# A float32 transformer kernel on one core: each 512-column matmul of the linear layers issued as two of 256 columns on the same weights

## What is computed

```python
proj = h @ w_in                                   # both mixing layers
out = mixed @ w_out
k, v = jnp.split(rms_norm(mem, mem_norm_g) @ w_kv, 2, axis=-1)      # 256 rows, not 512

def swiglu_ffn(x, norm_g, w_in, w_out):           # D_FF = 2816, four times
    gate, up = jnp.split(rms_norm(x, norm_g) @ w_in, 2, axis=-1)
    return (jax.nn.silu(gate) * up) @ w_out
```

## Time and profile before

| | |
|---|---|
| median of 3 runs | 3417.19 us (3414.03 to 3419.39) |
| profiled execution, whole | 3432.71 us |
| profiled execution, span from first to last instruction | 3430.7 us |
| PE busy | 3310.2 us, 18,526 matmuls |
| PEld busy | 2629.9 us, 18,526 weight loads |
| DVE, ACT, POOL busy | 1745.3, 1193.3, 411.6 us |
| mean granted TensorE clock | 0.980 of full |

### The profile page before, as it was taken

How to read it: one execution, slowest core, us unless ns; L and a number is a source line. 1 busy time by engine, 2 the same in 40 slices (tenths; PEclk the granted TensorE clock), 3 DMA queues, 4 the chain that set the end, 5 groups by cost and what they waited for, 6 DMA issues and landing times.

```text
span 3430.7 us, 44407 instructions
## 1 busy us (share of the span) xinstructions
PE 3310.2 (96%) x18526; PEld 2629.9 (77%) x18526; DVE 1745.3 (51%) x2533; ACT 1193.3 (35%) x1884; POOL 411.6 (12%) x318
## 2 busy tenths in 40 slices
PE   6999999899999999999999999999999999999999
PEld 5776778676677888887777778888877887678887
DVE  6854455744446644336767554433454334454333
ACT  3334432433443432224323342222343223342221
POOL 0000010000001311002322111100101011011110
PEclk9999999899999999999999999999999999899999
DMA  5631122221122333233200013332322333013332
GB/s 210 213 110 61 57 95 87 77 87 56 59 77 68 111 105 98 94 97 120 68 14 2 27 44 121 98 94 92 102 76 93 98 94 94 10 56 98 98 96 89
DMA packets 83911, 295.47 MB, mean 86 GB/s; under 512 B 9472, under 2 KB 12800, under 8 KB 81664
## 3 DMA queue, kind: packets, MB, share of 16 engines
q1 hardware_dynamic: 78384, 270.61, 24.7%
q10 hardware_dynamic: 5328, 22.02, 2.0%
HBM read 283.94 MB, written 8.65 MB: 85 GB/s over the span
## 4 chain that ended last, share of the span: by engine, by line
PE 84%; DVE 8%; ACT 2%; issue 2%; POOL 1%; DMA 0%; DVEq 0%; POOLq 0%; ACTq 0%
PE acc L476 66%; PE acc L1502 1%; DVE w_lo L387 1%; PE acc L3255 1%; PE acc L2481 1%; PE aux L3219 1%; DVE square_sums L2940 1%; PE aux L1783 1%; PE aux L3224 1%; PE acc L1814 1%; ACT w_hi L380 1%; DVE ssd_ex L1404 1%; PE acc L2485 1%; PE acc L2471 1%; PE aux L1801 1%
## 5 line engine op out<-in xcount | busy, mean ns | idle before, releaser
L476 PE MATMUL acc<-op_hi,w_hi 128*128 128x512 f32 x2624 | 1088.8, 415 | 32.7 <-DVE w_lo L387 18.3
L380 ACT ACTIVATE w_hi<-raw 128x1024 fp32r<-128x1024 f32 (+2 forms) x476 | 494.8, 1039 | 1542.2 <-PE acc L476 1513.6
L476 PE MATMUL acc<-op_hi,w_lo 128*128 128x512 f32 x2624 | 1030.5, 393 | 0.0
L476 PE MATMUL acc<-op_lo,w_hi 128*128 128x512 f32 x2624 | 1029.9, 392 | 0.0
L387 DVE TENSOR_TENSOR w_lo<-raw,w_hi 128x1024 fp32r<-128x1024 f32 (+2 forms) x476 | 577.0, 1212 | 297.0 <-ACT w_hi L380 296.6
L476 PEld LDWEIGHTS acc<-op_hi,w_hi 128*128 128x128 f32 x2624 | 496.7, 189 | 198.1 <-issue 72.8
L476 PEld LDWEIGHTS acc<-op_hi,w_lo 128*128 128x128 f32 x2624 | 496.4, 189 | 108.7
L476 PEld LDWEIGHTS acc<-op_lo,w_hi 128*128 128x128 f32 x2624 | 498.0, 190 | 102.3 <-issue 10.1
L476 PE MATMUL acc<-ffn_hi,w_hi 128*128 128x512 f32 x800 | 311.4, 389 | 0.0
L476 PE MATMUL acc<-ffn_lo,w_hi 128*128 128x512 f32 x800 | 311.2, 389 | 0.0
L476 PE MATMUL acc<-ffn_hi,w_lo 128*128 128x512 f32 x800 | 311.2, 389 | 0.0
(11 more groups left out here) (583 smaller groups left out, 3907.5 us busy)
## 6 DMA issues: line engine op xcount, KB each, us to landing
raw<-in_w SPq DMA_DIRECT2D x436, 512.0 KB, 3.5
late_ada<-in_ada ACTq DMA_DIRECT2D x32, 512.0 KB, 4.4
raw<-in_w SPq DMA_DIRECT2D x32, 384.0 KB, 3.1
ada<-in_ada ACTq DMA_DIRECT2D x4, 1024.0 KB, 14.3
ada<-in_ada SPq DMA_DIRECT2D x4, 1024.0 KB, 21.7
x_mid<-x SPq DMA_DIRECT2D x16, 256.0 KB, 3.3
x<-x_mid SPq DMA_DIRECT2D x2, 2048.0 KB, 7.9
skew<-rel_rows SPq DMA_DIRECT2D x12, 192.0 KB, 2.9
```

Source lines behind the costliest of these rows:

```text
L380: act.activation(self.w_hi[g % 2][:, 0:k, :], self.raw[s][:, 0:k, :], ACT.Copy).then_inc(self.split_hi.handle, 1)
L476: mm = pe.matmul(self.bank(s, g), w[:, k, :], a[:, k, 0:s.n], start=(k == 0 and q == 0), stop=(k == k_tiles - 1 and q == 2))
```

## The change

The three matmuls of a block become six: for each of the three products the first 256 columns, then the last 256, with the same weights and into the two halves of the same bank. The flag that opens an accumulation is set on the very first only, and the one that closes it on the very last only.

```diff
+STREAM = T // 2
+ROW = 128
 ...
-                hi, lo = s.moving
+                (hi, lo), bank = s.moving, self.bank(s, g)
 ...
                     for q, (w, a) in enumerate(((w_hi, hi), (w_hi, lo), (w_lo, hi))):
-                        mm = pe.matmul(self.bank(s, g), w[:, k, :], a[:, k, 0:s.n],
-                                       start=(k == 0 and q == 0), stop=(k == k_tiles - 1 and q == 2))
+                        for at in range(0, s.n, STREAM):
+                            mm = pe.matmul(bank[:, at:at + STREAM], w[:, k, :], a[:, k, at:at + STREAM],
+                                           start=(k == 0 and q == 0 and at == 0),
+                                           stop=(k == k_tiles - 1 and q == 2 and at + STREAM == s.n))
 ...
-        core.map_memory((nc.sbuf_base + 63) // 64 * 64 - X_AT * 1024)
+        core.map_memory((nc.sbuf_base + ROW - 1) // ROW * ROW - X_AT * 1024)
```

## The result

| | before | after |
|---|---|---|
| median | 3418.29 us (4 runs, 3414.03 to 3423.64) | 3531.35 us (4 runs, 3528.16 to 3540.07) |
| profiled span | 3430.7 us | 3526.1 us |
| matmuls, weight loads on PE | 18,526 each | 29,470 each |
| mean granted clock, profiled run | 0.980 | 0.988 |

The ratio of the times is 1.0321 (95% interval 1.0299 to 1.0344): the split makes the kernel 113 us slower. The two profiled spans differ by only 95 us, because the profiled run of before was an unlucky one: 3432.71 us at a clock of 0.980, where 31 other runs of the same kernel had 0.980 to 0.987, 0.985 in the mean. So sizes are taken as differences of medians, and the traces are used for the prices of single steps.

What follows compares the result with a forecast made beforehand. The linear layers' matmuls on PE were taken as the bound. 10,864 pairs at 12.7 ns gave 138 us gross, 126 after stalls; 3417.2 + 126 = 3543 us, 3.7% slower, range 3524 to 3570 for 8 in 10.

Steps and rivals of the forecast that it cites:

- Count, loads for kept weights: Linear layers on PE: 10,944 matmuls each become two, each with a load; keeping weights skips no load, gives no discount.
- Price of a pair, 12.1 to 13.3 ns, from the memory's stretch: Linear-layer matmuls: the memory's 256-column steps of 0.1194 us make a pair 12.1 to 13.3 ns dearer; 12.7 taken.
- Half clock, no cost: Half-clock stretches: 512 columns take 0.43 us, 256 take 0.21, so a split is free; some 80 matmuls, 10,864 left.
- What hides: PE's stalls in scans, for ACT or start-up transfers: about 10% of L476 is filler, so of 138 us gross 126 remain.
- Time at half clock: Whole kernel: 137 us at half clock before, mean clock 0.980; granted clock expected near 0.98 after the change.
- The load alone doesn't set the new step, but leaves 7 ns under it: PE's 256-column steps: loads are spaced 0.112 us, below the 0.1194 step, leaving only 7 ns.
- No change: Rival, 3%: the excess belongs to a change of weights, so the second half pays none; a pair 226.7 ns, 3417 us.
- faster: Rival, 3%: loads get ahead and both halves stream nearly bare; at most 145 us gained, at half of that 3344 us.
- small excess: Rival, 4%: the second half, on the same weights, pays say a fifth of the 13.4 ns; 29 us, 3446 us.
- The clock: Rival, 4%: 137 us more at half clock, where 256-column matmuls take longer, would cost 60 us; about 3603 us.
- Instructions: Rival, 3%: some 87 more instruction packets on PE, each 2.0 us late, add up to 174 us; 3717 us.
- What the profile would show: Changed kernel's profile: feed-forward steps of 0.12 us, slightly shorter PE waits, PEld's busy share from 77% to nearly all.

Runs made afterwards that it cites:

- the alternating kernel: The changed kernel with loops over halves and products swapped, all three products of the first half before the second half's; 3533.86 us, ratio 1.0332.
- e8: Kernel before, 512 columns, with the low-weight product moved second and computed for only 64 of 128 output features; 3439.98 us, ratio 1.0061.
- e9: The kernel of e8 with its matmuls in halves of 256 columns; 3490.23 us, ratio 1.0215.

## Why the prediction was right, point by point

- *Count, loads for kept weights.* Right: 10,944 more matmuls and loads, no skipped load and no discount (the alternating kernel, 3534).
- *Price of a pair, 12.1 to 13.3 ns, from the memory's stretch.* Right: 120 ns a step, 13.2 ns a pair in an unbroken stream, 12.8 over the dense stretches of the trace, and 12.9 by time in the feed-forward blocks. The memory's matmuls were the changed form itself, in the trace from the start, and reading them was enough.
- *Half clock, no cost.* The median step is 213 ns there, two of which are 427 as before. Right.
- *What hides.* This is the step that was mis-sized, and its mechanism was only half of the story. I took 138 us gross and let stalls swallow 12, for 126. At full clock the traces have 119: waits swallowed about 8, and some 11 are missing inside the bursts, which the prediction priced like an unbroken stream. The first product behind another stage's matmul costs 4 ns more in halves, not 13, and the second to twelfth 8.6 more, as they were slow already as whole matmuls. Undone part by part: 12.9 ns a pair in the feed-forward blocks, 6.8 elsewhere. Why whole F32R matmuls are slow behind a break and halves aren't is not settled; that they are is in the two traces, and e8 and e9 show the like in a dense stretch.
- *Time at half clock.* The sum held it constant. It fell a little: the four runs after have a clock of 0.985 to 0.988, the 31 before 0.980 to 0.987. In these 31 the time grows by 0.4 us for each us at half clock, so by estimate the 10 us less between the means (0.985 and 0.9865) are worth 4. Whether the change did that or chance, four runs can't tell. 119 less 4 is 115, and 113 was measured.
- *The load alone doesn't set the new step, but leaves 7 ns under it.* Right at 256 columns, and not far from the edge: with 128 columns next to 384 the load sets the time of the pair.
- *The rivals.* No change and faster need a cheaper second half: no step shows one. The size of the small excess is bfloat16's. The clock did not fall. Instructions came in time: 85 packets more, and a chain of 3294 matmuls without a break.
- *What the profile would show.* Loads' busy share rose from 77% to 91%, and PE's waits for `w_lo` shrank from 19.8 to 15.8 us.

The forecast of 3543 us was 12 us high over the measured 3531: about 7 by the term for what hides, and the rest mostly by less time at half clock. The gross sum was right for its reason. That 126 came so near owes something to luck, since a price a little too low (12.7 for 13.2) and the stalls' share a little too high made up for much of the discount that nobody had seen.

## What to carry to other kernels

A price per matmul can often be read in the trace of before, if any stage already runs the new form: here 192 matmuls of 256 columns gave the step to within a nanosecond, while a general figure would have given a fifth of the loss or even a gain. In F32R, don't cut a 512-column matmul when nothing is won by it: 6% on each in a dense stream, and far more as soon as the columns no longer cover the next load. And a price read in a uniform stream is an upper bound where stages are interleaved: check one burst of the mixed stage by itself, against the same place before.

If 16 bits of each operand are enough, bfloat16 parts with whole matmuls beat both kernels: 3290 us, 3.8% under the kernel before.

## What the runs showed of the hardware that I had not expected

- The excess over the columns is 13.4 ns for F32R and about 2.5 ns for bfloat16, at 512 and at 256 columns alike, at full clock.
- Behind a break in the stream an F32R product of 512 columns takes 230.6 ns instead of 226.9 for about a dozen products; in halves it doesn't (239.1 against 240.2), nor in bfloat16 (215.8 in both places).
- An F32R load of 128 columns of weights runs at the array's clock: steps of 111 ns at full and 213 ns at half clock when it is what binds.
- The records of PE can be without a gap and the granted clock still be half: 0.802 on average with 128-column matmuls, 0.980 to 0.990 in all other runs.
- With one product in three on 64 columns of weights (and in another order), a block of three 512-column products goes from 681 to 689 ns, and the same block in halves from 720 to 707.
